# Latent-head attention scores: one full-precision product replaced by three products of high and low parts

## The reference

```python
def mla_branch(c_q, c_kv, k_rope_raw, q_norm_g, w_uq, kv_norm_g, w_ukv, qh_g, kh_g, cos, sin):
    q = (rms_norm(c_q, q_norm_g) @ w_uq).reshape(b, s, MLA_HEADS, MLA_QK)
    kv = (rms_norm(c_kv, kv_norm_g) @ w_ukv).reshape(b, s, MLA_HEADS, MLA_NOPE + MLA_V)
    ...
    q = rms_norm(q, qh_g)
    k = rms_norm(k, kh_g)
    ...
    o = block_attention(q, k, v)

def block_attention(q, k, v):
    ...
        sc = jnp.einsum('bqgrd,bkgd->bgrqk', qi, k, preferred_element_type=jnp.float32) * scale
        p = jax.nn.softmax(sc, axis=-1).astype(v.dtype)
        return jnp.einsum('bgrqk,bkgv->bqgrv', p, v)
```

## Time and profile before

| | us |
|---|---|
| median of 3 runs | 1489.45 (1488.47 to 1489.49) |
| time of the profiled execution | 1489.07 |
| span in its profile, first to last instruction | 1487.2 |
| PE busy | 1471.3 (99%) |
| PEld busy | 1236.7 (83%) |
| DVE busy | 1101.9 (74%) |
| ACT busy | 884.2 (59%) |
| POOL busy | 60.5 (4%) |

### The profile page before, as it was taken

How to read it: one execution, slowest core, us unless ns; L and a number is a source line. 1 busy time by engine, 2 the same in 40 slices (tenths; PEclk the granted TensorE clock), 3 DMA queues, 4 the chain that set the end, 5 groups by cost and what they waited for, 6 DMA issues and landing times.

```text
span 1487.2 us, 20139 instructions
## 1 busy us (share of the span) xinstructions
PE 1471.3 (99%) x7808; PEld 1236.7 (83%) x7808; DVE 1101.9 (74%) x1673; ACT 884.2 (59%) x1348; POOL 60.5 (4%) x69
## 2 busy tenths in 40 slices
PE   8999999999999999999999999999999999999998
PEld 7877788888897778888888877888888888888886
DVE  6898778996578978699956767875467566887446
ACT  6565657775446555677744576664456455666435
POOL 1110000000021000000000001000000000100001
PEclk9999999999999999999999999999999999999999
DMA  7643446666655435566666523766646544566562
GB/s 253 193 143 118 150 155 190 203 190 189 192 164 170 135 112 179 156 198 192 187 191 204 171 100 114 224 190 190 196 156 234 166 121 138 166 196 194 187 193 76
DMA packets 73567, 255.70 MB, mean 172 GB/s; under 512 B 8448, under 2 KB 10112, under 8 KB 73472
## 3 DMA queue, kind: packets, MB, share of 16 engines
q1 hardware_dynamic: 73184, 254.25, 54.6%
q10 hardware_dynamic: 288, 0.17, 0.1%
HBM read 253.34 MB, written 1.05 MB: 171 GB/s over the span
## 4 chain that ended last, share of the span: by engine, by line
PE 93%; DVE 3%; ACT 2%; issue 1%; DMA 0%; POOL 0%; ACTq 0%; DVEq 0%
PE psum L1229 19%; PE psum L1256 18%; PE psum L1258 18%; PE psum L1260 18%; PE psum L1235 10%; PE psum L1188 4%; PE psum L1406 2%; DVE w_low L2170 1%; PE psum L1436 1%; PE psum L1504 1%; ACT w_high L1659 1%; PE psum L1249 1%; PE psum L1247 1%; PE psum L1250 1%; PE psum L1554 0%
## 5 line engine op out<-in xcount | busy, mean ns | idle before, releaser
L2170 DVE TENSOR_TENSOR w_low<-w_raw,w_high 128x1024 fp32r<-128x1024 f32 (+2 forms) x480 | 574.0, 1203 | 206.7 <-ACT w_high L1659 205.2
L1659 ACT ACTIVATE w_high<-w_raw 128x1024 fp32r<-128x1024 f32 (+2 forms) x480 | 498.3, 1042 | 243.7 <-PE psum L1260 212.0
L1229 PE MATMUL psum<-x_parts,w_high 128*128 128x512 f32 x992 | 248.8, 393 | 0.0
L1229 PEld LDWEIGHTS psum<-x_parts,w_high 128*128 128x128 f32 x992 | 178.6, 189 | 32.1
L1256 PE MATMUL psum<-w_high,x_parts 128*128 128x512 f32 (+2 forms) x432 | 171.1, 396 | 1.6 <-DVE w_low L2170 1.1
L1258 PE MATMUL psum<-w_low,x_parts 128*128 128x512 f32 (+2 forms) x432 | 164.9, 382 | 0.0
L1260 PE MATMUL psum<-w_high,x_parts 128*128 128x512 f32 (+2 forms) x432 | 164.7, 381 | 0.0
L1235 PEld LDWEIGHTS psum<-x_parts,w_low 128*128 128x128 f32 x992 | 135.3, 190 | 9.7
L1235 PE MATMUL psum<-x_parts,w_low 128*128 128x256 f32 x992 | 138.3, 282 | 0.0
L1256 PE MATMUL psum<-w_high,ff_high 128*128 128x512 f32 x256 | 100.0, 391 | 0.0
L1258 PE MATMUL psum<-w_low,ff_high 128*128 128x512 f32 x256 | 99.6, 389 | 0.0
(11 more groups left out here) (279 smaller groups left out, 2327.3 us busy)
## 6 DMA issues: line engine op xcount, KB each, us to landing
w_raw<-in_weights SPq DMA_DIRECT2D x450, 512.0 KB, 3.6
w_raw<-in_weights SPq DMA_DIRECT2D x16, 384.0 KB, 3.0
w_raw<-in_weights SPq DMA_DIRECT2D x8, 416.0 KB, 4.1
rows<-in_second_rows SPq DMA_DIRECT2D x4, 512.0 KB, 5.0
w_raw<-in_weights SPq DMA_DIRECT2D x6, 256.0 KB, 2.7
dil_masks<-in_consts SPq DMA_DIRECT2D x1, 768.0 KB, 6.5
residual<-in_x SPq DMA_DIRECT2D x2, 256.0 KB, 4.3
residual<-in_x SPq DMA_DIRECT2D x1, 512.0 KB, 6.3
```

The costliest lines, as they stand in the source:

```text
L1229: eng.matmul(acc[:, f * PANEL:(f + 1) * PANEL], wh[:, j, f * P:(f + 1) * P], parts[:, k, :, :].rearrange("p s n -> p (s n)"), start=k == 0 ...
L1659: act(self.unit_view(self.wh, u), raw, ACT.Copy).then_inc(sem("w_high"), 1)
L2170: tt(self.unit_view(self.wl, u), raw, self.unit_view(self.wh, u), ALU.subtract).then_inc(sem("w_low"), 1)
```

## The change

The one tile `mla_heads` becomes two, `mla_heads_high` and `mla_heads_low`, both float32r and both double-buffered over the latent pairs. In each of the steps `mla_turn_k` and `mla_turn_q` ScalarE now copies the bank out with the gain, rounded to float32r (the high part), and VectorE then forms bank times gain minus the high part (the low part), waiting for ScalarE. Only the low part's semaphore (`m_k_taken`, `m_q_taken`) lets TensorE go on. Each score product becomes three that accumulate in the same bank: high by high, high by low, low by high.

```diff
--- before.py
+++ after.py
@@ -918,7 +918,8 @@
             m["mq"], m["mk"] = (tok[:, i * n:(i + 1) * n].rearrange("p (t h d) -> p t h d", t=TT, h=MLA_H)
                                 for i in range(2))
             m["kd"] = tok[:, 0:2 * TT * GQA_KV * HD].rearrange("p (t g u d) -> p t g u d", t=TT, g=GQA_KV, u=2)
-            m["qk"] = by_tile(sb("mla_heads", 2 * MLA_H * SEQ))
+
+            m["heads"] = [by_tile(sb(f"mla_heads_{i}", 8 * SEQ, F32R)) for i in ("high", "low")]
             m["gh"] = by_tile(sb("gqa_heads", (GQA_H // 2 + GQA_KV) * SEQ))
             m["mv"] = sb("mla_v", TT * MLA_H * MLA_V).rearrange("p (t h d) -> p t h d", t=TT, h=MLA_H)
             m["gqk"] = sb("gqa_tokens", TT * (GQA_H + GQA_KV) * HD).rearrange("p (t h d) -> p t h d", t=TT, d=HD)
@@ -1398,13 +1399,17 @@
                     p = n - GQA_H // 2
                     q.wait_ge(sem("m_k_taken"), at("mla_turn_k", l, p))
                     q.wait_ge(sem("m_q_taken"), at("mla_turn_q", l, p))
-                    qt = [m["qk"][0:MLA_QK, 2 * p + i, :] for i in range(2)]
-                    kt = [m["qk"][0:MLA_QK, MLA_H + 2 * p + i, :] for i in range(2)]
+                    (qt, kt), (q_low, k_low) = ([self.latent(l, p, part, what) for what in "qk"] for part in range(2))
                 for i in range(2):
                     acquire(4 + i)
                     for t in range(TT):
-                        d = eng.matmul(bank[4 + i][:, t * SEQ:(t + 1) * SEQ], qt[i][:, t * P:(t + 1) * P], kt[i],
-                                       start=True, stop=True)
+                        o, c = bank[4 + i][:, t * SEQ:(t + 1) * SEQ], slice(t * P, (t + 1) * P)
+                        if n < GQA_H // 2:
+                            d = eng.matmul(o, qt[i][:, c], kt[i], start=True, stop=True)
+                        else:
+                            eng.matmul(o, qt[:, i, c], kt[:, i, :], start=True, stop=False)
+                            eng.matmul(o, qt[:, i, c], k_low[:, i, :], start=False, stop=False)
+                            d = eng.matmul(o, q_low[:, i, c], kt[:, i, :], start=False, stop=True)
                     d.then_inc(sem("scored"), 1)
                     free[4 + i] = (sem("exp_done"), 2 * (at("p_exp", l, n) - 1) + i + 1)
 
@@ -1761,12 +1766,12 @@
                     act(o.rearrange("p (t h d) -> p t h d", t=TT, h=MLA_H), tile, ACT.Square
                         ).then_inc(sem("m_squared"), 1)
 
-            elif kind == "mla_turn_q":
+            elif kind in ("mla_turn_k", "mla_turn_q"):
                 l, p = key
-                q.wait_ge(sem("m_q_turned"), at(*step))
-                act(self.mix[l]["qk"][0:MLA_QK, 2 * p:2 * p + 2, :],
-                    bank[5][0:MLA_QK, :].rearrange("p (k s) -> p k s", k=2), ACT.Copy,
-                    scale=self.first_col(l, "q_head_g")[0:MLA_QK, :]).then_inc(sem("m_q_taken"), 1)
+                what, b = kind[-1], 5 if kind == "mla_turn_q" else 7
+                q.wait_ge(sem(f"m_{what}_turned"), at(*step))
+                act(self.latent(l, p, 0, what), bank[b][0:MLA_QK, :].rearrange("p (k s) -> p k s", k=2), ACT.Copy,
+                    scale=self.first_col(l, what + "_head_g")[0:MLA_QK, :]).then_inc(sem(f"m_{what}_high"), 1)
 
             elif kind == "take_mq":
                 l, panel = key
@@ -2048,6 +2053,11 @@
                 j, = key
                 q.wait_ge(sem("dil_headed"), at("dil_av", TT * j + 1))
                 split_high(in_order(self.dil_out[0][:, j, :]), to_order(bank[7][:, 0:SEQ]), "dil_high")
+
+    def latent(self, l, p, part, what):
+
+        at = p % 2 * 4 + 2 * "qk".index(what)
+        return self.mix[l]["heads"][part][0:MLA_QK, at:at + 2, :]
 
     def head_stat(self, n, i):
         at = 128 + 32 * (n % 2) + 16 * i
@@ -2357,12 +2367,13 @@
             elif kind == "window_mean":
                 self.window_means(q, eng, key[0])
 
-            elif kind == "mla_turn_k":
+            elif kind in ("mla_turn_k", "mla_turn_q"):
                 l, p = key
-                q.wait_ge(sem("m_k_turned"), at(*step))
-                ts(self.mix[l]["qk"][0:MLA_QK, MLA_H + 2 * p:MLA_H + 2 * p + 2, :],
-                   bank[7][0:MLA_QK, :].rearrange("p (k s) -> p k s", k=2), self.first_col(l, "k_head_g")[0:MLA_QK, :],
-                   None, ALU.mult).then_inc(sem("m_k_taken"), 1)
+                what, b = kind[-1], 5 if kind == "mla_turn_q" else 7
+                q.wait_ge(sem(f"m_{what}_high"), at(*step))
+                stt(self.latent(l, p, 1, what), bank[b][0:MLA_QK, :].rearrange("p (k s) -> p k s", k=2),
+                    self.first_col(l, what + "_head_g")[0:MLA_QK, :], self.latent(l, p, 0, what), ALU.mult, ALU.subtract
+                    ).then_inc(sem(f"m_{what}_taken"), 1)
 
             elif kind == "take_gates":
                 l, panel = key
```

## The result

The changed kernel takes **1496.39 us** (median of four runs, 1495.89 to 1497.36) against 1489.37 (1488.47 to 1489.49) for the one before: ratio 1.0049, 95% interval 1.0037 to 1.0061. The forecast was 1495.4, within 1491.8 to 1499.5, "slower" at 80%. The profiled execution took 1495.89.

What follows compares the result with a forecast made beforehand. A nearly gapless TensorE stream bounds the kernel; waits for low parts less the saving add 2.96 us a layer, 5.9 for two, taking the profiled 1489.07 to 1495.0; with 0.4 for the median, 1495.4 us, range 1491.8 to 1499.5.

Steps and rivals of the forecast that it cites:

- The saving: Latent scores on TensorE: twelve float32r products 0.12 us apart replace four float32 ones, 0.30 us a pair, 2.4 in all.
- The low part: VectorE's subtraction for the keys or queries of a latent pair: 0.74 us at 512 columns.
- The bounds of 0.69 and 0.95: Limits for a low part: ScalarE's pass over the same bank, 0.69 us, and twice the 256-column row, 0.95.
- the row with a gain column: Profile row of the same VectorE form at 256 columns: 0.475 us, where the skill's formula gives 0.424.
- The path: Query low part, serial behind ScalarE's copy and VectorE's queue: scores of pairs 1 to 3 late by 0.52, 2.74, 3.26 us.
- the 0.9, 2.7 and 1.0 that I said it would show: Sign: TensorE's waits in us for VectorE's low part ahead of the scores of pairs 1, 2 and 3, both layers.
- What was next in line: Transposes of the attention weights: some 0.1 us left in pair 2 before they wait for normalised weights, so nothing added.
- The clock: Rival, 8%: TensorE's clock falls behind two stands of 2.5 us, some 4 us each beyond the stand; 1503 us.
- the one at the start: Slow-clock stretch of TensorE around the kernel's start, 1.2 before 2.4 GHz, taken to last some 8 us.
- Not in time: Rival, 10%: low parts of the queries come in time, so only the saving is left; 1487.1 us.
- A fixed small wait: Rival, 17%: VectorE catches up each round and six later pairs cost one low part each, 0.79 us; 1491.8 us.
- A dearer low part: Rival, 10%: low parts take 0.95 us, or the weights' transposes wait too; 1498 us.

Runs made afterwards that it cites:

- experiment 1: Changed kernel without low parts: all three products of a score use high parts and TensorE waits for ScalarE's high copies alone; 1486.85 us, ratio 0.9984.
- experiment 3: Changed kernel with the copies of finished gates panels put behind the step that turns the queries; 1493.77 us, ratio 1.0029.
- 5: Changed kernel with the queries turned one head unit earlier; 1493.9 us, ratio 1.0034.
- 7: Changed kernel with the queries turned one head unit earlier and the pooled windows two rounds later; 1492.03 us, ratio 1.0017.
- Experiment 2: Changed kernel with low parts made from the high tile but neither read nor waited for; 1489.59 us, ratio 1.0003.
- experiment 4: Changed kernel with nine unused 512-column products on TensorE ahead of the scores of pair 2; 1494.96 us, ratio 1.0039.
- Experiment 6: Changed kernel with the pooled windows moved two rounds later; 1496.45 us, ratio 1.0051.
- 8: Kernel before the change, with queries turned one head unit earlier and pooled windows two rounds later; 1492.58 us, ratio 1.0022.

## Why the prediction was right, point by point

**The saving.** Right: 0.12 between products; 2.4 us forecast, 2.3 in the trace of experiment 1 and 2.6 in its median.

**The low part.** Forecast 0.74, measured 0.74 to 0.75. The bounds of 0.69 and 0.95 weren't needed; that VectorE can't be quicker than ScalarE's pass, as the lower one has it, no run shows. The Trainium skill's 0.69 (VectorE: DVE Perf Modes, The TRN2 errata) is 0.05 short here, as it was for the row with a gain column.

**The path.** The score starts came 0.54, 2.62 and 3.16 us late where 0.52, 2.74 and 3.26 were worked out, and a layer costs 2.87 (2.96). Pair 2 came out 0.1 shorter (VectorE is 1.01 us late at its reciprocal, 134.14 plus 0.54 against 133.67, where 1.13 were counted), and pair 0 of the second layer 0.2 dearer, where the forecast had nothing: the two make up for each other, so that the 5.9 for both layers fits better than its parts. That the low part is serial to the query copy and stands behind `w_low` and `gates` is what experiments 3, 5 and 7 show: without the `gates` ahead the delay of pair 2 is 1.07, with the early turn no wait for a low part is left. The waits as the profile counts them, 0.7, 2.3 and 0.7, are below the 0.9, 2.7 and 1.0 that I said it would show: a bracket begins at the modelled end of the last transpose, which lies behind the moment at which the next product could have started. Counted from 0.79 behind the first of the eight transposes, where the scores of pair 0 in layer 1 start, TensorE stands for 0.97, 2.53 and 0.97.

**What was next in line.** The forecast left the weights' transposes 0.1 us in pair 2 and charged nothing. That holds for the changed kernel. Experiment 2 shows what lies under it: some 3.1 us, in pair 3 more than in pair 2, which comes up as soon as the query's wait is gone and the pooling work stays.

**The clock.** This is the term that is missing. The median is 1.0 us above the forecast; the fall cost 1.57 in the profiled execution and 1.4 by experiment 4 (1496.39 less 1494.96). That the miss is not larger is in part luck: the profiled execution began 0.54 us earlier than the one before. I had the fall as a rival, 8%, two of them at "some 4 us" each. In the profiled execution there was one, and it cost 1.6: the low stretch was shorter than the one at the start, from which I took its length. The execution of 1497.36 has a mean granted clock of 0.997 where the other three have 0.999, so it may have had a further fall; it left no trace. The chance was too low as well; the range held because a fall is cheap.

**The rivals.** Not in time: six waits show it. A fixed small wait: refuted by pair 2, though experiment 3 came near to it. A dearer low part: refuted by its 0.74, and no wait at the weights' transposes is in the list of the changed kernel.

## What to carry to other kernels

Before an operation is split into parts that other engines make, look who ends its wait today. If it already starts behind a copy, each further step on the operand is added to the path with the queue of the engine that does it, and the saving of 0.3 us stands against that. What cured it here was an earlier step (a faster one was not tried): move up what feeds it, only where its bank is free, and take out of the queue what nobody waits for; then time the kernel before with the same moves, or their cost and their gain are put down to the change.

When a queue is cleared, the wait comes back one consumer further on (weights' transposes, exponentials, `x_parts`); each was named in the sorted waits of the run that cleared the one before.

## What the runs showed of the hardware

The granted clock fell behind some stands of TensorE and not behind others of the same length. Of seven stands of some 2 us in the profiled executions (changed kernel 2.28 and 2.27, experiment 6 2.05 twice, 5, 7 and 8 1.98 each), four were followed by a stretch at 1.2 GHz: the second of the changed kernel, the first of 6, and those of 7 and 8. TensorE was busy right before and right after each of the seven. Experiment 6 in layer 1:

```profile
136.00:140.00 4.00, 1.95 (x16) 1.61 (x15) 3.59 (x6) 2.59 (x4) 0.00 (x0) 0.98 0.35 91
140.00:144.00 4.00, 4.00 (x18) 3.68 (x17) 2.38 (x5) 1.65 (x7) 0.00 (x0) 0.59 0.12 46
```

Each such stretch cost about 1.6 us beside its stand (1.57 in the changed kernel and in 6; 1.61 in 7 and in 8, against the same place in 5, which has the stand and not the fall), and filling the stand with unread products took it away (experiment 4). Other executions differ from the profiled ones: of the eleven of 7, seven have a mean granted clock of 0.998 and took 1492.02 to 1492.3, the profiled one has 0.999 and took 1491.29. The Trainium skill (TensorE: Matmul & The Clock Gate, Why this matters for your kernels) warns that idle gaps bring the half clock back; the traces agree for four of the seven stands, and all seven are shorter than the gaps that it warns of. Why one of two stands of equal length brings it and the other doesn't stays open.
